# The delta net's transposed inverse factor, made by transposing instead of by a second product

## The chip, the core and the metric

The kernel runs on one core of one Trainium2 chip. The metric is device time in microseconds. The core's engines are named as the profile names them: PE is TensorE (PEld its weight loads), DVE VectorE, ACT ScalarE, POOL GpSimd, SP the queue that issues most DMAs. All data is float32.

## The reference, cut to what matters

The model is one block with a delta net and a gated linear attention, a mixture of experts, and two transformer layers, for 256 tokens and a context of 256 more. The change touches only the solve inside the delta net:

```python
kb = k * beta[..., None]
a = jnp.where(strict, jnp.einsum('nbhik,nbhjk->nbhij', kb, k) * decay, 0.0)
rhs = jnp.concatenate([v * beta[..., None], kb * jnp.exp(gcum)[..., None]], axis=-1)
sol = lax.linalg.triangular_solve(a, rhs, left_side=True, lower=True, unit_diagonal=True)
u, w = sol[..., :dv], sol[..., dv:]
```

So for each head and chunk the inverse of a unit triangular matrix, I + a, is applied to two right sides. The scan over the chunks then carries a state of 128x128 per head. It is done for 4 heads in two directions.

## The kernel before, in words

The kernel works with chunks of 128 tokens, so there are 4 chunks (two of the context, two of the sequence), 2 directions `d` and 4 heads. A step is `(d, s, phase)`: direction, place of the chunk in the scan, and one of ten phases. Four heads are always handled together: "a four" below is the four products of 128x128 by 128x128 that the helper `four` issues into one PSUM bank, or four transposes into one bank. Bank `AB[d]` (2 or 3) and bank `CD[d]` (4 or 5) belong to direction `d`.

The inverse is built by doubling. `B[0]` holds a block diagonal inverse X, and `B[3]` its transpose Y. Phase 1 makes both for blocks of 2. Each of phases 2 to 7 doubles the blocks:

- POOL masks the matrix into `B[4]` (line 1980, event `dn_am`).
- PE makes the four P = B4'B0 into `AB` (`dn_p`), and ACT copies it to `B[5]` (line 2195, `dn_p_copied`).
- PE makes the four "X product", B3'B5, into `AB` (`dn_x`, line 853, not in phase 7, where X is no longer needed), and the four "Y product", B5'B3, into `CD` (`dn_y`, line 854).
- DVE subtracts the X product from `B[0]` (line 1483, `dn_xs`) and the Y product from `B[3]` (line 1485, `dn_ys`).

Phase 0 makes the matrix (`dn_segments`, `dn_gram`, on DVE line 1443), phase 8 uses Y for w and u and the product with the state (`dn_w`, `dn_u`, `dn_ws`), phase 9 makes the state update and the output.

The order is written out by hand in `DN_SLOTS`: 44 slots; in slot t direction 0 is at phase t mod 10 and direction 1 four slots behind it. Below, slot (5,1) means direction 0 at phase 5 and direction 1 at phase 1. In a slot every engine does `delta_first` of direction 0, then of direction 1, then `delta_second` of each, then its `fill_slot`. Every engine works strictly in its own order. The fills are work of other parts that covers waits: projections of the layer's input on PE in slots 0 to 6 (512 or 256 columns a product, 7 us a slot), and on DVE convolutions in slots 1 and 2, a head norm in slot 3 and smaller pieces in 4 and 5. After slot 6 there is no fill, and with direction 0 finished in slot 39 the last four slots have direction 1 alone.

Phase 1 on DVE is four operations on SBUF operands in a row (lines 1191, 1449, 1191, 1453): X for blocks of 2, then its transpose. For s = 2 and 3 there are three more in `delta_second` (1191 three times), which make the score matrix of the output. POOL has one or two operations a slot and direction: the mask of line 1980, and products of keys, values or gates (line 1957) in phases 3, 5, 6 and 7.

All matrix products are recorded under line 501 and all transposes under line 513, the helpers' lines. All copies by ACT are under line 2010.

Of the kernel before, what the change touches and what calls it, by code (L numbers as in the profile page):

```python
# [20 lines left out]
ALU = mybir.AluOpType  # L21
# [12 lines left out]
H = 4  # L34
# [91 lines left out]
def dn_count(*phases, chunks=range(4)):  # L126

    steps = [step for slot in DN_SLOTS for step in slot if step[2] in phases and step[1] in chunks]
    return {step: i + 1 for i, step in enumerate(steps)}


DN_0, DN_1, DN_8, DN_9 = (dn_count(phase) for phase in (0, 1, 8, 9))
DN_1Q = dn_count(1, chunks=(2, 3))
# [112 lines left out]
def build(nc, A, out):  # L246
    with ExitStack() as ctx:
# [239 lines left out]
        def _(engine):  # L487
# [295 lines left out]
            def delta_first(step):  # L783
# [17 lines left out]
                elif phase < 8:  # L801
# [3 lines left out]
                    else:  # L805
                        engine.wait_ge(*pe.at("dn_x0", DN_1[d, s, 1]))
                        if s >= 2:
                            engine.wait_ge(*pe.at("dn_q3_copied", DN_1Q[d, s, 1]))
                    four(AB[d], d, lambda m, h: (B[4][:, m, :], B[0][:, m, :]), "dn_p")
                elif phase == 8:  # L810
                    engine.wait_ge(*pe.at("dn_ys", DN_LEVELS[d, s, 7]))
                    engine.wait_ge(*pe.at("dn_kb", DN_KB[d, s, 3]))
# [20 lines left out]
            def delta_second(step):  # L833
# [10 lines left out]
                elif 2 <= phase < 8:  # L844
                    engine.wait_ge(*pe.at("dn_p_copied", DN_LEVELS[step]))
                    if phase > 2:
                        engine.wait_ge(*pe.at("dn_ys", DN_LEVELS[d, s, phase - 1]))
                    else:
                        engine.wait_ge(*pe.at("dn_y0", DN_1[d, s, 1]))
                        if s >= 2:  # L850
                            engine.wait_ge(*pe.at("dn_q2_copied", DN_1Q[d, s, 1]))
                    if phase < 7:
                        four(AB[d], d, lambda m, h: (B[3][:, m, :], B[5][:, m, :]), "dn_x")
                    four(CD[d], d, lambda m, h: (B[5][:, m, :], B[3][:, m, :]), "dn_y")
                elif phase == 8 and s:
# [330 lines left out]
        def _(engine):  # L1186
# [247 lines left out]
            def delta_first(step):  # L1434
# [10 lines left out]
                elif phase == 1:  # L1445
# [6 lines left out]
                    engine.wait_ge(*v.last())  # L1452
                    tt(of(B[3], d), wide(ident), of(B[3], d), ALU.subtract).then_inc(*v.inc("dn_y0"))
                elif phase == 9 and s < 3:
                    engine.wait_ge(*v.at("dn_ds", DN_S[step]))
# [11 lines left out]
            def delta_second(step):  # L1467
# [12 lines left out]
                elif 2 <= phase < 8:  # L1480
                    if phase < 7:
                        engine.wait_ge(*v.at("dn_x", DN_XS[step]))
                        tt(of(B[0], d), of(B[0], d), ps(2 + d), ALU.subtract).then_inc(*v.inc("dn_xs"))
                    engine.wait_ge(*v.at("dn_y", DN_LEVELS[step]))
                    tt(of(B[3], d), of(B[3], d), ps(4 + d), ALU.subtract).then_inc(*v.inc("dn_ys"))  # L1485
                elif phase == 8 and s:
# [1026 lines left out]
```

## Time and profile before

| | us |
|---|---|
| median of 3 runs | 2779.77 |
| lowest and highest run | 2775.85, 2779.93 |
| span of the profiled execution, first to last instruction | 2773.7 |
| median of the runs less that span (start and end of the launch, and the spread between executions) | 6.1 |
| the delta net's 44 slots in the profile | about 302 to 556 |
| PE, DVE, ACT, POOL busy in the whole span | 92%, 40%, 21%, 4% |
| mean granted TensorE clock, as a share of full speed | 0.963 |

The page has no total of the profiled execution itself beside its span. Busy shares are averages over parts with different limits; what counts for this change is the stretch from 302 to 556 us. "PEclk" is the granted clock of TensorE: 1.00 is 2.4 GHz and 0.50 is 1.2 GHz. In the groups, the idle time behind a bar or in square brackets is the engine's idle time before the work, with what ended it.

### The profile page before, as it was taken

To read this page: it belongs to the slowest core of one execution; us is meant where nothing else is said; L and a number is where in the kernel's file an instruction comes from. 1 tells how busy PE (TensorE), PEld (TensorE's weight loads), DVE (VectorE), ACT (ScalarE), POOL (GpSimd) and SP (SyncE) were. 2 spreads that over 40 slices of the span, in tenths; PEclk is the share of its full clock that TensorE was granted. 3 is DMA by queue.
4 is the path that set the end of the run, shared out by engine and by line. 5 is a ranking of instruction groups with operands and counts; after the bars stand their busy time and mean duration, and the time that the engine had idled before them with its cause. 6 is when DMAs were issued, how large, how long until landed. Compare 5 with 4: busy or idle time off the path is not lost.

```text
span 2773.7 us, 37722 instructions
## 1 busy us (share of the span) xinstructions
PE 2550.8 (92%) x15259; PEld 1933.4 (70%) x15264; DVE 1103.4 (40%) x2325; ACT 585.4 (21%) x1032; POOL 115.3 (4%) x98
## 2 busy tenths in 40 slices
PE   5999889989799999979999779999999997799998
PEld 2686588868456655549948468699499484586993
DVE  1455445501311111136550831366666507312665
ACT  3632422210211111121011521110100105311000
POOL 0000144300000000000000000000000000000000
PEclk8999999999999999989999889999999998799999
DMA  7126100025499999974444004344344350043340
GB/s 280 62 79 278 54 31 1 1 108 211 157 414 422 422 422 422 422 309 173 178 147 173 30 1 182 152 166 184 142 162 176 144 196 31 1 182 152 153 168 15
DMA packets 74309, 485.50 MB, mean 175 GB/s; under 512 B 7872, under 2 KB 14528, under 8 KB 16704
## 3 DMA queue, kind: packets, MB, share of 16 engines
q1 hardware_dynamic: 65808, 472.46, 42.8%
q10 hardware_dynamic: 8368, 11.14, 1.2%
q8 instruction: 98, 1.61, 0.2%
q14 instruction: 35, 0.29, 0.0%
HBM read 479.38 MB, written 4.19 MB: 174 GB/s over the span
## 4 chain that ended last, share of the span: by engine, by line
PE 82%; DVE 7%; DMA 5%; ACT 3%; issue 2%; SPq 0%; ACTq 0%; DVEq 0%; POOL 0%; POOLq 0%
PE bank L501 80%; DMA ring<-in_stream 5%; ACT arena L2010 2%; PE bank L513 2%; DVE arena L1191 1%; DVE softmax_small L1881 1%; DVE arena L1879 1%; DVE arena L1902 0%; ACT hT L2010 0%; DMA bias_scratch<-arena 0%; ACT ring_late L2010 0%; DVE arena L1449 0%; ACT L2010 0%; DVE softmax_small L1889 0%; DVE arena L1485 0%
## 5 line engine op out<-in xcount | busy, mean ns | idle before, releaser
L501 PE MATMUL bank<-arena 128*128 128x128 f32 (+4 forms) x3864 | 619.5, 318 | 67.8 <-ACT arena L2010 43.1
L501 PEld LDWEIGHTS bank<-arena 128*128 128x128 f32 (+2 forms) x3864 | 485.4, 195 | 175.5 <-issue 87.0
L501 PE MATMUL bank<-hT,ring 128*128 128x256 f32 (+2 forms) x2144 | 463.3, 374 | 8.1 <-issue 6.7
L2010 ACT ACTIVATE arena<-bank 128x512 f32<-128x512 f32 (+2 forms) x384 | 218.0, 568 | 1156.7 <-PE bank L501 1131.2
L501 PEld LDWEIGHTS bank<-hT,ring 128*128 128x128 f32 x2144 | 357.5, 193 | 97.1 <-issue 64.7
L501 PE MATMUL bank<-ring,arena 128*64 128x256 f32 (+3 forms) x2184 | 298.6, 406 | 31.3 <-DMA ring<-in_stream 29.0
L501 PE MATMUL bank<-hT,ring_late 128*128 128x256 f32 (+1 forms) x1568 | 279.4, 336 | 6.7 <-issue 6.7
L501 PEld LDWEIGHTS bank<-ring,arena 128*64 128x64 f32 (+2 forms) x2184 | 176.4, 141 | 144.7 <-issue 82.7
L501 PEld LDWEIGHTS bank<-hT,ring_late 128*128 128x128 f32 x1568 | 248.9, 193 | 31.0 <-issue 7.5
L2010 ACT ACTIVATE hT<-bank 128x256 f32<-128x256 f32 (+2 forms) x92 | 38.6, 420 | 642.4 <-PE bank L501 471.3
L501 PE MATMUL bank<-arena,ring_late 128*128 128x128 f32 (+1 forms) x1088 | 157.4, 299 | 5.1 <-DVE arena L1485 2.8
L501 PE MATMUL bank<-ring_late,hT 128*64 128x512 f32 (+2 forms) x632 | 162.0, 584 | 0.0
L1191 DVE TENSOR_TENSOR arena<-arena 128x512 f32<-128x512 f32 (+5 forms) x55 | 33.7, 615 | 321.4 <-ACT arena L2010 320.8
L501 PEld LDWEIGHTS bank<-arena,ring_late 128*128 128x128 f32 x1088 | 144.2, 193 | 12.7 <-DVE arena L1485 3.6
L513 PE MATMUL bank<-constants,arena 128*128 128x128 f32 x492 | 87.1, 325 | 58.3 <-ACT arena L2010 44.5
L501 PE MATMUL bank<-arena,ring 128*128 128x128 f32 (+1 forms) x864 | 125.0, 299 | 11.5 <-issue 8.0
L513 PEld LDWEIGHTS bank<-constants,arena 128*128 128x128 f32 x492 | 68.1, 167 | 93.1 <-issue 58.0
L1191 DVE TENSOR_TENSOR arena<-arena,bank 128x512 f32<-128x512 f32 x16 | 11.0, 688 | 303.7 <-PE bank L501 303.7
L501 PEld LDWEIGHTS bank<-arena,ring 128*128 128x128 f32 x864 | 114.1, 195 | 17.7 <-issue 12.7
L501 PEld LDWEIGHTS bank<-ring_late,hT 128*64 128x64 f32 (+1 forms) x632 | 58.1, 147 | 87.8 <-issue 85.0
L501 PE MATMUL bank<-ring_late,arena 128*64 128x256 f32 (+2 forms) x680 | 115.7, 404 | 3.2 <-DVE arena L1513 2.3
L2001 POOL TENSOR_TENSOR x_tok<-x_tok,arena 128x512 f32<-128x512 f32 x8 | 11.8, 1492 | 2207.2 <-DVE arena L1802 2207.2
(215 smaller groups left out, 2239.1 us busy)
## 6 DMA issues: line engine op xcount, KB each, us to landing
ring<-in_stream SPq DMA_DIRECT2D x248, 1024.0 KB, 8.9
ring_late<-in_stream SPq DMA_DIRECT2D x198, 1024.0 KB, 10.4
arena<-bias_scratch ACTq DMA_DIRECT2D x4, 1536.0 KB, 18.0
bias_scratch<-arena ACTq DMA_DIRECT2D x12, 256.0 KB, 2.0
constants<-in_con SPq DMA_DIRECT2D x1, 1184.0 KB, 9.3
x_tok<-in_x SPq DMA_DIRECT2D x1, 1024.0 KB, 5.3
arena<-in_ctx SPq DMA_DIRECT2D x1, 1024.0 KB, 6.8
out<-x_tok SPq DMA_DIRECT2D x2, 512.0 KB, 2.7
```

The lines of the kernel that those rows point to most:

```text
L501: ins = engine.matmul(out_, lhsT, rhs, start=start, stop=stop, skip_group_check=True)
L513: ins = engine.transpose(out_, in_, ident[0:k, 0:k])
L1191: return tt(o, x, y, ALU.mult)
L1879: tt(e, src, bias2[:, m.bias], ALU.add).then_inc(*v.inc("sm_in"))
L1881: engine.tensor_reduce(stat(m, 0), e, AX.X, ALU.max).then_inc(*v.inc())
L2001: engine.tensor_tensor(x, x, ffU[j], ALU.add).then_inc(*g.inc("ff_joined"))
L2010: engine.activation(o, i, f, **kw).then_inc(*s_.inc(ev))
```

## The change

In phases 2 to 6 the Y product and its subtraction are gone. Instead, in phases 3 to 7 PE transposes X (`B[0]`, as the phase before left it) right behind the P product, with four transposes into bank `CD[d]`, and DVE copies the bank to `B[3]`. Phase 7 still has the Y product and its subtraction, which start from the transposed X. `DN_Y` numbers the events: `turned` for a transpose and its copy, `last` for the product of phase 7. The copy stands in DVE's `delta_first`, so it comes after what DVE's fill of the slot before has, and after what direction 0 has in `delta_first` when it belongs to direction 1.

```diff
+DN_Y = dn_y_count()
@@ PE, delta_first, phases 2 to 7
                     four(AB[d], d, lambda m, h: (B[4][:, m, :], B[0][:, m, :]), "dn_p")
+                    if phase > 2:
+                        if phase > 3:
+                            engine.wait_ge(*pe.at("dn_ys", DN_Y[d, s, phase - 1, "turned"]))
+                        for h in range(H):
+                            transpose(CD[d][:, 128 * h:128 * h + 128], B[0][:, 4 * d + h, :], ev="dn_y" if h == H - 1 else None)
                 elif phase == 8:
-                    engine.wait_ge(*pe.at("dn_ys", DN_LEVELS[d, s, 7]))
+                    engine.wait_ge(*pe.at("dn_ys", DN_Y[d, s, 7, "last"]))
@@ PE, delta_second, phases 2 to 7
                     if phase > 2:
-                        engine.wait_ge(*pe.at("dn_ys", DN_LEVELS[d, s, phase - 1]))
+                        engine.wait_ge(*pe.at("dn_ys", DN_Y[d, s, phase, "turned"]))
...
                     if phase < 7:
                         four(AB[d], d, lambda m, h: (B[3][:, m, :], B[5][:, m, :]), "dn_x")
-                    four(CD[d], d, lambda m, h: (B[5][:, m, :], B[3][:, m, :]), "dn_y")
+                    else:
+                        four(CD[d], d, lambda m, h: (B[5][:, m, :], B[3][:, m, :]), "dn_y")
@@ DVE, delta_first
+                elif 3 <= phase < 8:
+                    engine.wait_ge(*v.at("dn_y", DN_Y[*step, "turned"]))
+                    engine.tensor_copy(of(B[3], d), ps(4 + d)).then_inc(*v.inc("dn_ys"))
@@ DVE, delta_second
                         tt(of(B[0], d), of(B[0], d), ps(2 + d), ALU.subtract).then_inc(*v.inc("dn_xs"))
-                    engine.wait_ge(*v.at("dn_y", DN_LEVELS[step]))
-                    tt(of(B[3], d), of(B[3], d), ps(4 + d), ALU.subtract).then_inc(*v.inc("dn_ys"))
+                    else:
+                        engine.wait_ge(*v.at("dn_y", DN_Y[*step, "last"]))
+                        tt(of(B[3], d), of(B[3], d), ps(4 + d), ALU.subtract).then_inc(*v.inc("dn_ys"))
```

Later lines move: the products' line 501 is 511 after the change, the transposes' 513 is 523, DVE's subtractions 1483 and 1485 are 1502 and 1505, phase 1's 1191, 1449 and 1453 are 1207, 1465 and 1469, the convolution's 1335, 1337 and 1339 are 1351, 1353 and 1355, and the copy is 1472.

PE before, from the fill of slot 2 through slot 3 (direction 0 alone, phase 3) into the fill of slot 3, whose transposes wait for `pj_free`:

```order
L501 MATMUL bank<-hT,ring 128x512 x7
L501 MATMUL bank<-arena 128x128 [waits dn_xs,dn_am]
L501 MATMUL bank<-arena 128x128 x3
L501 MATMUL bank<-arena 128x128 [waits dn_ys,dn_p_copied]
L501 MATMUL bank<-arena 128x128 x7
L513 MATMUL bank<-constants,arena 128x128 [waits pj_free]
```

PE after, the same place:

```order
L511 MATMUL bank<-hT,ring 128x512 x7
L511 MATMUL bank<-arena 128x128 [waits dn_xs,dn_am]
L511 MATMUL bank<-arena 128x128 x3
L523 MATMUL bank<-constants,arena 128x128 x4
L511 MATMUL bank<-arena 128x128 [waits dn_ys,dn_p_copied]
L511 MATMUL bank<-arena 128x128 x3
L523 MATMUL bank<-constants,arena 128x128 [waits pj_free]
```

Four of the eight products behind the wait are gone, and four transposes stand between P and that wait.

DVE before, the end of slot 2's work and slot 3's (the second convolution, 1335 to 1339, is the fill of slot 2; the head norm follows):

```order
L1485 TENSOR_TENSOR arena<-arena,bank 128x512 [waits dn_y]
L1335 TENSOR_SCALAR ring_late<-ring_late,vectors 128x512 [waits pj_free]
L1337 SCALAR_TENSOR_TENSOR ring_late<-ring_late,vectors 128x2x255 [waits dve]
L1339 SCALAR_TENSOR_TENSOR ring_late<-ring_late,vectors 128x2x255 [waits dve]
L1483 TENSOR_TENSOR arena<-arena,bank 128x512 [waits dn_x]
```

DVE after:

```order
L1351 TENSOR_SCALAR ring_late<-ring_late,vectors 128x512 [waits pj_free]
L1353 SCALAR_TENSOR_TENSOR ring_late<-ring_late,vectors 128x2x255 [waits dve]
L1355 SCALAR_TENSOR_TENSOR ring_late<-ring_late,vectors 128x2x255 [waits dve]
L1472 COPY arena<-bank 128x512 [waits dn_y]
L1502 TENSOR_TENSOR arena<-arena,bank 128x512 [waits dn_x]
```

What the X product waits for (`dn_ys`) stood ahead of the convolution, and stands behind it now.

DVE before, slot (5,1): the end of slot (4,0), phase 1 of direction 1, and direction 0's subtractions of phase 5:

```order
L1485 TENSOR_TENSOR arena<-arena,bank 128x512 [waits dn_y]
L1191 TENSOR_TENSOR arena<-arena,constants 128x512 [waits dn_a]
L1449 TENSOR_TENSOR arena<-constants,arena 128x512 [waits dve]
L1191 TENSOR_TENSOR arena<-arena,constants 128x512 [waits dn_at_copied]
L1453 TENSOR_TENSOR arena<-constants,arena 128x512 [waits dve]
L1483 TENSOR_TENSOR arena<-arena,bank 128x512 [waits dn_x]
```

DVE after:

```order
L1472 COPY arena<-bank 128x512 [waits dn_y]
L1207 TENSOR_TENSOR arena<-arena,constants 128x512 [waits dn_a]
L1465 TENSOR_TENSOR arena<-constants,arena 128x512 [waits dve]
L1207 TENSOR_TENSOR arena<-arena,constants 128x512 [waits dn_at_copied]
L1469 TENSOR_TENSOR arena<-constants,arena 128x512 [waits dve]
L1502 TENSOR_TENSOR arena<-arena,bank 128x512 [waits dn_x]
```

Ahead of phase 1's four operations there is now a copy that waits for transposes of the same slot, where there was a subtraction of the slot before. In slot (1,7) the copy stands behind the four operations instead, and the Y product of direction 1 waits for it.

## Rows read from the trace of the kernel before

**Rows 1.** Busy time by stretch: us, busy (instructions) by engine, PEclk, DMA share, GB/s.
```profile
305.40:556.00 250.60, 225.47 (x1687) 204.07 (x1690) 131.60 (x204) 68.11 (x108) 96.36 (x76) 0.99 0.04 16
```
**Rows 2.** Groups by shape, 305 to 562 us: busy, mean ns | idle before.
```profile
L501 PE MATMUL bank<-arena 128*128 128x128 f32 x1288 | 162.3, 282 | 20.4 <-ACT arena L2010 13.5 <-DVE arena L1483 4.7 <-DVE arena L1489 0.8
...
L1459 DVE COPY arena<-bank 128x512 f32<-128x512 f32 x2 | 1.4, 692 | 1.5 <-PE bank L501 1.5
```
**Rows 3.** Timeline (start, length): four transposes, then a four of products.
```profile
385.59 0.60 PE L513 MATMUL bank<-constants,arena 128*128 128x128 f32 x4
386.02 1.06 PE L501 MATMUL bank<-arena 128*128 128x128 f32 x8
```
**Rows 4.** Timeline: two fours without a wait between them, ACT's copy of the first.
```profile
421.76 1.06 PE L501 MATMUL bank<-arena,ring_late 128*128 128x128 f32 x8
422.65 1.06 PE L501 MATMUL bank<-ring_late,arena 128*128 128x128 f32 x8
422.92 0.60 ACT L2010 ACTIVATE arena<-bank 128x512 f32<-128x512 f32 x1 [3.10 <-PE bank L501]
```
**Rows 5.** Timeline, direction 1 alone, phases 5 to 6.
```profile
539.65 0.60 ACT L2010 ACTIVATE arena<-bank 128x512 f32<-128x512 f32 x1 [4.88 <-PE bank L501]
540.30 3.16 PE L501 MATMUL bank<-arena 128*128 128x128 f32 x24 [0.75 <-ACT arena L2010]
541.50 0.69 DVE L1483 TENSOR_TENSOR arena<-arena,bank 128x512 f32<-128x512 f32 x1 [3.90 <-PE bank L501]
543.56 0.60 ACT L2010 ACTIVATE arena<-bank 128x512 f32<-128x512 f32 x1 [3.31 <-PE bank L501]
```
**Rows 6.** Timeline, slot 3: PE's P and products, the convolution's end on DVE.
```profile
325.86 1.05 PE L501 MATMUL bank<-arena 128*128 128x128 f32 x8
327.66 2.05 PE L501 MATMUL bank<-arena 128*128 128x128 f32 x16 [0.75 <-ACT arena L2010]
328.96 0.75 DVE L1339 SCALAR_TENSOR_TENSOR ring_late<-ring_late,vectors 128x510 f32<-128x510 f32 x1
329.55 1.04 PE L513 MATMUL bank<-constants,arena 128*128 128x128 f32 x8
```
**Rows 7.** Timeline, slot (5,1) of s = 2 into slot (6,2).
```profile
458.23 0.68 DVE L1191 TENSOR_TENSOR arena<-arena,constants 128x512 f32<-128x512 f32 x1
458.92 1.28 POOL L1980 TENSOR_TENSOR arena<-arena,constants 128x512 f32<-128x512 f32 x1 [2.53 <-PE bank L501]
458.94 1.80 DVE L1449 TENSOR_TENSOR arena<-constants,arena 128x512 f32<-128x512 f32 x1
463.79 0.67 DVE L1483 TENSOR_TENSOR arena<-arena,bank 128x512 f32<-128x512 f32 x1
464.61 10.30 PE L501 MATMUL bank<-arena 128*128 128x128 f32 x88 [1.19 <-DVE arena L1483]
```
**Rows 8.** Timeline, slots (1,7) and (2,8), direction 0 at s = 2.
```profile
438.79 0.69 DVE L1449 TENSOR_TENSOR arena<-constants,arena 128x512 f32<-128x512 f32 x1
440.12 1.64 DVE L1453 TENSOR_TENSOR arena<-constants,arena 128x512 f32<-128x512 f32 x1
443.61 0.68 DVE L1485 TENSOR_TENSOR arena<-arena,bank 128x512 f32<-128x512 f32 x1
444.34 1.16 PE L501 MATMUL bank<-arena,ring_late 128*128 128x128 f32 x8 [1.02 <-DVE arena L1485]
```
**Rows 9.** PE's two longest waits here, and PE by stretch (columns of rows 1).
```profile
335.37 3.24 PE L501 MATMUL bank<-arena 128*128 128x128 f32 x16 [2.04 <-ACT arena L2010]
410.12 11.81 PE L501 MATMUL bank<-arena 128*128 128x128 f32 x88 [2.96 <-DVE arena L1483]
...
411.20:414.60 3.40, 3.40 (x18) 0.51 0.00 0
414.60:418.00 3.40, 3.40 (x33) 1.00 0.02 5
```
**Rows 10.** PE in a stretch with 16 transposes of v, fill of slot 5.
```profile
350.52 1.04 PE L513 MATMUL bank<-constants,ring_late 128*128 128x128 f32 x8
350.00:360.00 10.00, 9.69 (x79) 1.00 0.03 13
```

More of the change, by code:

```diff
@@ L129, in dn_count, with dn_y_count @@
     return {step: i + 1 for i, step in enumerate(steps)}
+def dn_y_count():
+    order = []
+    for slot in DN_SLOTS:
+        order += [(*step, "turned") for step in slot if 3 <= step[2] < 8]
+        order += [(*step, "last") for step in slot if step[2] == 7]
+    return {key: i + 1 for i, key in enumerate(order)}
+DN_Y = dn_y_count()
 DN_0, DN_1, DN_8, DN_9 = (dn_count(phase) for phase in (0, 1, 8, 9))
```

## The prediction, made before the change was run

> **What bounds the kernel now.** The busy shares come first, and mislead a little: PE is busy for 92% of the whole span, so less PE work looks like a gain. The change acts only in the delta net, so I read the stretch of its slots. From 305.4 to 556 us PE is busy for 225.5 of 250.6 us [rows 1]. The groups by shape say what ended PE's idle time there: 13.5 us ACT's copies of P, 4.7 us DVE's X subtraction, all before products of this solve [rows 2]. So PE is the bound where both directions have work, and the chain P, copy, X product, subtraction, next P is the bound where one direction has nothing beside it. The timeline gives that chain's lengths, and the windows the clock.
>
> **The steps, from rows.** A four of products takes PE 0.89 us (421.76 to 422.65), and its reader starts 1.16 after its start on ACT [rows 4] and 1.20 on DVE after a wait of PE (540.30 to 541.50) [rows 5]. A four that PE has waited for takes 0.1 more. A four of transposes takes PE 0.43 (385.59 to 386.02) and is 4 records where a four of products is 8 [rows 3]. I take 0.20 from the end of a four to DVE's start, which is 1.20 less 0.99, and 0.05 from the end of a copy to PE (539.65 + 0.60 to 540.30) [rows 5], 0.15 from the X subtraction (463.79 + 0.67 to 464.61) [rows 7]. DVE's copy of a bank takes 0.69 [rows 2], as its subtraction does [rows 5]. DVE's busy time therefore stays: 40 subtractions go and 40 copies come.
>
> Removed on PE: phases 2 to 6, 4 chunks, 2 directions, 40 fours of 0.89, 35.6 us. Added: phases 3 to 7, 40 fours of 0.43, 17.2 us. PE does 18.4 us less. That would be the gain if PE never waited.
>
> On the transposes' price the Trainium skill (TensorE: Matmul & The Clock Gate, Terms) says that TensorE's transpose mode is four times faster for FP32. By that a four would take 0.22 and PE would save 8 us more; the row shows a factor of two, and the row is used.
>
> **What the new order costs.** The X product waits for the copy of the transposed X, and that starts only when P and the transposes are through. P to X alone was 1.81 (1.16 + 0.60 + 0.05). After a wait it becomes 0.99 + 0.43 + 0.20 + 0.69 + 0.05 = 2.36. Behind X nothing of its own follows any more: before, Y's 0.89 covered the subtraction. Now X to the next P of that direction is 1.20 + 0.69 + 0.15 = 2.04, of which X itself covers 0.99. So the Y product's time comes back as a wait wherever the other direction has no four behind X.
>
> Slot by slot, in 3 turns of 10 slots, a first part with fills and a tail:
>
> 1. Slots 2 to 6, where PE is full of fills. Slot 2 loses Y: -0.89. In slot 3 DVE's copy stands behind the convolution of the fill, which ends at 329.71 (328.96 + 0.75) [rows 6]. It follows an ACT copy at the end of PE's fill, so it moves with PE to 328.8; copy and start put X at 329.55, its end at 330.45. Before, X and Y ended at 329.44. That is +1.0 in sum, +1.9 for the slot. Slots 4 and 5 wait for ACT, which is busy with other work, longer than for the copy, and lose Y: -0.89 each. Slot 6 loses two Y and gains one four of transposes: -1.35. Together -2.1.
> 2. Slots (8,4), (9,5), (0,6): the other direction's fours stand behind X, so the Y product's 0.89 is gained and 0.43 to 0.48 paid: -0.45, -0.3, -0.4. Three turns and one more (8,4): -3.9.
> 3. Slots (3,9) and (4,0): X is last, own P is next. Saved 0.89, paid 0.43 for the transposes and 1.05 of wait less the 0.1 to 0.3 that is there now: +0.45 each, 6 of them: +2.8.
> 4. Slot (5,1) into (6,2). DVE's phase 1 begins after the copy. From P of phase 5 (about 457.7, 1.2 ahead of POOL's start) to P of phase 6 it is 6.9 now, of which phase 1 takes 5.56 (458.23 to 463.79) [rows 7]. It then begins 2.31 after P instead of 0.5. Its length depends on POOL: where POOL starts during it the second operation takes 1.80 [rows 7], where not 0.69, and the four take 3.7 (0.72 more than 438.79 to 441.76) [rows 8]. Starting later, it meets less of POOL's two operations. I take 5.0 between 3.7 and 5.6, nearer to the collided row because POOL's second operation of the slot is then still running. P of phase 6 comes at 2.31 + 5.0 + 0.82 = 8.1 (6.8 to 8.7), +1.2; slot (6,2) does 1.35 less work and waits 0.15 more. Net 0.0 a turn, between -1.3 and +0.6.
> 5. Slots (1,7), (2,8). Direction 1's copy stands behind phase 1 of direction 0, its Y product behind the copy. For s = 1 the last subtraction came right after phase 1; now copy 0.74 and Y 1.19 stand between, +1.9, less the 0.89 of Y in slot (2,8): +1.0. For s = 2, 3 three more DVE operations cover Y (441.76 to 443.61) [rows 8]: +0.65 for the copy in DVE's queue, less 0.89: about 0. PE waits here anyway (1.02 at 444.34).
> 6. Slot (7,3): two fours of transposes for one Y: +0.1 in each of 4.
> 7. The tail, direction 1 alone, phases 5 to 7: a step is 3.91 (539.65 to 543.56) [rows 5] and becomes 2.36 + 2.04 = 4.4. Three steps: +1.4.
>
> Sum: -2.1 - 3.9 + 2.8 + 0.0 + 1.0 + 0.4 + 1.4 = -0.4.
>
> **The clock.** In this stretch it fell twice to 1.2 GHz, after PE had waited 2.04 and 2.96. In the 3.40 us behind the second wait PE did 18 records where it does 33 at 2.4 GHz [rows 9]: 15 records of 0.111, 1.7 us. It did not fall after 1.19 [rows 7]. The change lengthens waits: slot 3 to about 3.2, slot (1,7) of s = 1 to 2.7, slot (6,2) to about 4.2 and 2.4 for s = 1 and 2. I take one fall more, +1.7; none to three is possible, 0 to +5.
>
> The forecast is +1.3 on the profiled span of 2773.7. The median of the runs is 6.1 above that span, and nothing outside the stretch changes, so 2779.77 + 1.3 = 2781.1. What a measurement of this kernel tells from no change is 0.2%, 5.6 us, so the forecast is no change that can be seen: the 18.4 us go into waits.
>
> **Rivals.**
>
> PE's time counts (faster). For it: PE is 90% busy in the stretch. Against: the waits that appear are in the chain of each direction. If phase 1 takes its shortest 3.7 in slot (5,1), and the (3,9) and (4,0) waits are half of what I say, the sum is -0.4 - 3.9 - 1.5 = -5.8 without a further fall: 2774. With every one of the 40 exchanges paying its 0.46 it would be -18.4, 2761; the tail alone excludes that.
>
> Phase 1 on DVE is the bound (slower). The place is slot (5,1) into (6,2), where the copy pushes phase 1 back while it still collides with POOL at 5.6 us, and the slots (1,7), where the copy stands behind it. The price is +0.6 a turn, 1.8, and a fall of the clock after each of the longer waits, three instead of one, 3.4 more: +6.5, 2786. It decides from two falls more than I count. For it: waits of 2.04 were enough once. Against: a shorter wait in slot (5,1) of s = 3 (no keys' product on POOL).
>
> The transposes let the clock fall (slower). If PE at transposes were as good as idle for the clock, each wait would grow by the 0.43 to 0.87 of transposes beside it and the waits of about 1 us would reach the 2.04 after which it fell. Five more falls are +8.5, with -0.4 that is 2788. Against: the stretch of 10 us with the 16 transposes of v had the clock at 1.00 throughout [rows 10], though they were only a fifth of its records. The Trainium skill (TensorE: Matmul & The Clock Gate, Part 4: PE-mode transpose) has this rule: transpose mode does not count as busy for the clock gate in the same way.
>
> **How the numbers follow.** The forecast has 0.50, "PE's time counts" 0.22, "phase 1 is the bound" 0.21, the transposes' clock 0.07. Of the 0.22 some 0.13 lie more than 5.6 us below, since its price of 5.8 is just at that bound. Of the 0.21 some 0.18 lie above it, all of the 0.07, and 0.05 of the forecast's own upper edge. So faster by over 0.2% 0.13, within 0.2% 0.57, slower 0.30. The range begins where phase 1 is shortest, the waits of item 3 are halved and one of the two falls of the clock goes too: 2779.77 - 5.8 - 1.7 = 2772.3, and ends with the transposes' clock at 2788 and 1 us beyond: 2772 to 2789. The forecast's own range is 2775 to 2785.
>
> **What would show it.** PE's busy time from 305 to 556 falls by 17 to 19 us and its idle time grows by as much. The transposes' group grows by 160 records at 0.11 of pitch. In slot 3 PE waits about 3 us for DVE's copy behind the convolution. The tail's step is 4.4. In slot (5,1) phase 1 starts 2.3 after P. PEclk shows three or four falls in the stretch. I am wrong if the transposes take 0.89, if the X product waits for ACT as before, or if the clock falls six times.

## The result, and the profile after

| | before | changed |
|---|---|---|
| median | 2775.62 us (20 runs, 2773.29 to 2779.93) | 2781.23 us (20 runs, 2776.31 to 2785.35) |
| ratio to before | 1 | 1.0018, interval 1.0012 to 1.0025 |
| span of the profiled execution | 2773.7 us | 2780.5 us |

The forecast of 2781.1 us was met. Its step was not: it was made as 1.3 us over a median of 3 runs, 2779.77, and in the 20 runs before has a median of 2775.62. The measured step is about +5 us (0.0018 x 2775.6; the two medians are 5.6 apart), with an interval of +3.3 to +6.9. What had to be explained is therefore not whether the sum was near, but where some 4 us more came from.

TensorE's groups by shape, 305 to 568 us of the changed kernel (they answer [rows 2]):

```profile
L511 PE MATMUL bank<-arena 128*128 128x128 f32 x974 | 135.1, 289 | 37.8 <-DVE arena L1472 17.5 <-DVE arena L1502 17.1 <-ACT arena L2030 2.3
L523 PE MATMUL bank<-constants,arena 128*128 128x128 f32 x232 | 35.4, 286 | 1.9 <-ACT arena L2030 1.9
```

The products before which PE was idle for 20.4 us [rows 2] are now ones before which it is idle for 37.8. ACT's copy of P, which ended 13.5 us of it, ends 2.3; the new copy of the transposed factor (L1472) ends 17.5 and the subtraction of X (L1502), which the Y product used to cover, 17.1 (4.7 before). The work removed has come back as two waits. VectorE's groups in the same stretch show that it has as many operations as before, 40 copies and 40 subtractions (and the 8 of phase 7):

```profile
L1472 DVE COPY arena<-bank 128x512 f32<-128x512 f32 x40 | 27.6, 690 | 55.3 <-PE bank L523 55.2
L1502 DVE TENSOR_TENSOR arena<-arena,bank 128x512 f32<-128x512 f32 x40 | 27.4, 684 | 32.5 <-PE bank L511 32.5
```

PE by stretch (the columns of [rows 1]): first the delta net's slots, then one fall of the clock, the 3.4 us behind it, and a long fall in the tail.

```profile
305.40:562.80 257.40, 215.84 (x1525) 191.51 (x1525) 127.72 (x204) 69.58 (x109) 94.06 (x76) 0.95 0.05 17
...
390.80:394.20 3.40, 3.40 (x20) 3.40 (x20) 0.69 (x1) 0.17 (x1) 0.18 (x1) 0.60 0.00 0
394.20:397.60 3.40, 2.53 (x23) 2.37 (x22) 0.69 (x1) 1.62 (x3) 2.08 (x2) 1.00 0.00 0
550.80:561.00 10.20, 8.55 (x40) 7.88 (x39) 1.38 (x2) 1.45 (x3) 0.00 (x0) 0.51 0.01 2
```

The slots have 162 records fewer than in [rows 1] (160 by the change, 40 x 8 less 40 x 4), yet end 6.8 us later. Of these 6.8 us, 5.3 arise in the solve and 1.5 ahead of it (below). In the window of [rows 1], 305.4 to 556 us, PE is busy for 210.6 us instead of 225.5: 14.9 less, where 17 to 19 were said, since work at 1.2 GHz takes longer. The first of the short stretches is mostly at 1.2 GHz (0.60 on the mean), the one behind it at 2.4; the last is at 1.2 GHz for all of its 10.2 us.

The timeline of the changed kernel at the places the prediction speaks of: slot 3 (answers to [rows 6]), the slots (0,6) and (1,7) of s = 1, slot (5,1) of s = 1 (to [rows 7]), the first P behind slot (2,8) of s = 1, and the tail (to [rows 5]).

```profile
329.58 0.75 DVE L1355 SCALAR_TENSOR_TENSOR ring_late<-ring_late,vectors 128x510 f32<-128x510 f32 x1
330.25 0.69 DVE L1472 COPY arena<-bank 128x512 f32<-128x512 f32 x1
331.08 1.13 PE L511 MATMUL bank<-arena 128*128 128x128 f32 x8 [3.11 <-DVE arena L1472]
...
380.36 1.28 ACT L2030 ACT_TABLE_LOAD   x1 [2.69 <-PE bank L511]
382.35 1.12 DVE L1459 SCALAR_TENSOR_TENSOR arena<-bank,arena 128x128 f32<-128x128 f32 x4 [2.21 <-ACT arena L2030]
383.39 0.68 DVE L1472 COPY arena<-bank 128x512 f32<-128x512 f32 x1
384.22 1.13 PE L511 MATMUL bank<-arena 128*128 128x128 f32 x8 [1.73 <-DVE arena L1472]
386.22 1.13 PE L511 MATMUL bank<-arena 128*128 128x128 f32 x8 [0.44 <-DVE arena L1502]
388.04 1.63 DVE L1469 TENSOR_TENSOR arena<-constants,arena 128x512 f32<-128x512 f32 x1
389.60 0.68 DVE L1472 COPY arena<-bank 128x512 f32<-128x512 f32 x1
390.43 3.51 PE L511 MATMUL bank<-arena 128*128 128x128 f32 x16 [2.64 <-DVE arena L1472]
...
397.49 1.13 PE L511 MATMUL bank<-arena 128*128 128x128 f32 x8 [0.87 <-DVE arena L1502]
...
407.15 1.13 PE L511 MATMUL bank<-arena 128*128 128x128 f32 x8 [1.01 <-DVE arena L1502]
409.36 0.82 DVE L1207 TENSOR_TENSOR arena<-arena,constants 128x512 f32<-128x512 f32 x1
...
413.82 0.68 DVE L1502 TENSOR_TENSOR arena<-arena,bank 128x512 f32<-128x512 f32 x1
414.64 1.19 PE L511 MATMUL bank<-arena 128*128 128x128 f32 x4 [3.92 <-DVE arena L1502]
...
545.96 1.13 PE L511 MATMUL bank<-arena 128*128 128x128 f32 x8 [0.87 <-DVE arena L1502]
548.41 1.13 PE L511 MATMUL bank<-arena 128*128 128x128 f32 x8 [0.88 <-DVE arena L1472]
550.41 1.91 PE L511 MATMUL bank<-arena 128*128 128x128 f32 x8 [0.87 <-DVE arena L1502]
```

In slot 3 and in (1,7) the copy starts as soon as the operation ahead of it in DVE's queue is through, and PE waits 3.11 and 2.64 us for it. In (0,6) of s = 1 it is behind the four operations of L1459 (1443 before), which make the matrix of the new chunk and themselves wait for ACT; and ACT is late because it first loads a table, 1.28 us. No other turn has such a load: in (0,6) of s = 2 the copy starts 0.20 us behind the transposes and X waits 0.88. In (5,1) phase 1 begins 2.21 us after P. The tail's step is 4.45 us (545.96 to 550.41), with two waits of 0.87 in it.

### The profile page after: what moved, and what is told of

It is laid out like the page before. It is cut to its first block, busy times and chain, and to the rows that moved or that the text cites. A ratio compares the mean times of both kernels' runs of the same rounds, so it can differ in the third digit from the quotient of the medians.

```text
span 2780.5 us, 37408 instructions
## 1 busy us (share of the span) xinstructions
PE 2543.8 (91%) x15104; PEld 1920.9 (69%) x15104; DVE 1100.1 (40%) x2325; ACT 585.1 (21%) x1032; POOL 113.0 (4%) x98
## 4 chain that ended last, share of the span: by engine, by line
PE 83%; DVE 8%; ACT 3%; DMA 3%; issue 2%; SPq 0%; ACTq 0%; DVEq 0%
PE bank L511 81%; DMA ring<-in_stream 3%; PE bank L523 2%; ACT arena L2030 2%; DVE arena L1207 1%; DVE softmax_small L1901 1%; DVE arena L1899 1%; DVE arena L1922 0%; DVE arena L1472 0%; DVE arena L1502 0%; ACT hT L2030 0%; DMA bias_scratch<-arena 0%; ACT ring_late L2030 0%; ACT L2030 0%; DVE arena L1465 0%
## 5 line engine op out<-in xcount | busy, mean ns | idle before, releaser
L511 PE MATMUL bank<-arena 128*128 128x128 f32 (+4 forms) x3544 | 591.7, 323 | 85.2 <-ACT arena L2030 32.3
L511 PEld LDWEIGHTS bank<-arena 128*128 128x128 f32 (+2 forms) x3544 | 455.3, 197 | 196.7 <-issue 111.4
L523 PE MATMUL bank<-constants,arena 128*128 128x128 f32 x652 | 111.1, 313 | 59.3 <-ACT arena L2030 43.5
L523 PEld LDWEIGHTS bank<-constants,arena 128*128 128x128 f32 x652 | 87.5, 161 | 93.0 <-issue 58.3
```

The lines of the kernel that those rows point to most:

```text
L511: ins = engine.matmul(out_, lhsT, rhs, start=start, stop=stop, skip_group_check=True)
L523: ins = engine.transpose(out_, in_, ident[0:k, 0:k])
```

## The experiments

All read the solve in one way. It is cut at the first product of phase 8 of a direction (the groups with `arena,ring_late` as operands, [rows 4] shows one at 421.76): from P of direction 0, phase 2, s = 0 to its phase 8 ("start"), from there from one phase 8 of direction 0 to the next (three turns), and from the last to phase 8 of direction 1 ("tail"). The falls of the clock to 1.2 GHz in each part are in brackets, read from windows of 0.4 us.

| solve in us | start | turn 1 | turn 2 | turn 3 | tail | sum |
|---|---|---|---|---|---|---|
| before | 54.66 (1) | 51.80 (1) | 52.99 | 56.48 | 18.82 | 234.75 |
| before, second profile | 54.66 (1) | 51.81 (1) | 52.98 | 56.49 | 18.82 | 234.76 |
| e12, before and busy | 54.03 | 50.31 | 52.98 | 56.49 | 18.83 | 232.64 |
| changed | 52.87 (1) | 55.46 (2) | 53.91 (1) | 55.63 | 22.18 (long) | 240.05 |
| e10, changed, second profile | 53.24 (1) | 54.19 (1) | 53.90 (1) | 55.64 | 20.07 | 237.04 |
| e2, Y kept in the tail | 53.26 (1) | 54.16 (1) | 53.91 (1) | 55.62 | 19.00 | 235.95 |
| e3, changed and busy | 54.24 (1) | 52.80 | 52.56 | 55.62 | 20.07 | 235.29 |
| e1, 19 places | 51.31 | 49.57 | 51.94 | 54.96 | 18.99 | 226.77 |
| e11, 19 places, second profile | 51.31 | 50.98 (1) | 51.97 | 54.98 | 19.00 | 228.24 |
| e5, the other 21 | 55.26 (1) | 56.42 (2) | 54.03 | 57.29 | 19.89 | 242.89 |
| e7, 22 places | 50.76 | 49.58 | 51.96 | 54.96 | 19.00 | 226.26 |
| e8, 22 places and busy | 51.78 | 49.58 | 51.95 | 54.96 | 19.00 | 227.27 |
| e4, identity | 54.53 (1) | 60.26 (2) | 56.39 | 59.52 | 21.90 | 252.60 |
| e6, turned twice | 56.68 (2) | 59.02 (2) | 56.26 | 59.33 | 21.82 | 253.11 |

Parts without a fall repeat to 0.03 us from one profile to another and between kernels that are alike there (the start, where transfers and fills run, to 0.4). So a term can be read part by part.

One difference lies ahead of the solve, in work that no edit touches. P of phase 2 starts at 315.30 and 315.05 us in the two profiles of before, and at 316.82 and 316.53 in those of the changed kernel, 1.5 later. About half of it is a fall of the clock near 300 us, before and changed:

```profile
301.60:304.60 3.00, 2.33 (x18) 1.85 (x16) 0.00 (x0) 2.94 (x4) 0.00 (x0) 1.00 0.33 87
...
301.60:304.60 3.00, 3.00 (x6) 1.28 (x5) 0.00 (x0) 2.16 (x3) 0.00 (x0) 0.50 0.00 0
```

All twelve other profiles have that fall, e12 too, whose solve is that of before. So it isn't the exchange that brings it; what does is not shown.

**e1 and e5: the two halves of the change.** Both name the set of places; phases outside it keep the Y product of the phase before.

```diff
+DN_TURN = {(d, s, p) ... if (d == 1 and p <= 6 and not (s == 3 and p == 6)) or (d == 0 and p == 7)}   # e5: not (...)
-                    if phase > 2:
+                    if step in DN_TURN:
                         ... transpose(CD[d][:, 128 * h:128 * h + 128], B[0][:, 4 * d + h, :], ...)
-                    else:
+                    if dn_product(step):       # phase 7, or the next phase is not in DN_TURN
                         four(CD[d], d, lambda m, h: (B[5][:, m, :], B[3][:, m, :]), "dn_y")
```

> The transposes stand only where the other direction's products lie behind X or where PE waits anyway: direction 1 in phases 3 to 6 (not in phase 6 of s = 3) and direction 0 in phase 7, 19 of the 40 places; elsewhere the Y product stays as before. Theory 'waits by place' (the order of the work decides): each turn keeps the -0.3 to -0.45 of slots (8,4), (9,5), (0,6) and loses the +0.45 of (3,9) and (4,0) and the +1.4 of the tail; about -2 a turn, -5 to -8 us against before (0.2 to 0.3%), -10 to -13 against the changed kernel where the falls of the clock go too. Theory 'clock': the waits of 2.6 and 3.9 us of s = 1 (direction 0 in slots (1,7) and (5,1)) are here too wherever the copy stands ahead of phase 1 on DVE, so at least two falls stay, and it is -2 to -4 against before. Theory 'transposes do not count for the clock': 19 places instead of 40, so about half of the changed kernel's extra falls, 0 to +2 against before.

> The complement of the kernel with 19 places: the transposes stand only in the other 21 (direction 0 in phases 3 to 6, direction 1 in phase 7 and in phase 6 of s = 3). If what each place costs adds up, this one is at the changed kernel less the 19 places: with 2781.2 for the changed kernel, 2775.1 for before and 2768.2 for the 19 places, +13 against before, 2788. By the waits alone (without the clock) the prediction's terms give less: +2.8 for (3,9) and (4,0), +1.0 for slot (1,7), +1.4 for the tail, -2.1 for the fills, so +3 and with three more falls of the clock +8. Under +3 would say that the gain of the 19 places isn't theirs.

Measured: e1 2768.18 us, ratio 0.9972 (0.9962 to 0.9982); e5 2785.63 us, ratio 1.0032 (1.0021 to 1.0043). One half is faster than before by 0.28%, the other slower by 0.32%. The ratios add up to +0.0004 where both together have +0.0018; with intervals of 0.0010 and 0.0011 to either side of the two, that is no clear difference. In the solve the parts without falls tell more: with before at 231.6 (e12 less 1.0, see there) e1 is at -4.9 and e5, its three falls taken off at 1.4 to 1.65 each, at +6.8; together +1.9, and the changed kernel is at +1.0 (below). So the halves add up to within 1 us. Of e1's 6.9 us, 4.9 are the order of the work. Its profile has no fall in the solve where before has two, worth 3.1 us, and lost 1.5 ahead of the solve. e5 is 9.1 us above the before of its runs, between the +8 of the waits with three falls and the +13 of the sum of places. PE in e1 by stretch, and two of its waits on the timeline:

```profile
330.00:360.00 30.00, 26.32 (x178) 23.62 (x177) 15.56 (x28) 13.53 (x17) 11.88 (x9) 1.00 0.17 63
...
405.00:425.00 20.00, 17.04 (x144) 16.27 (x144) 11.76 (x18) 4.18 (x7) 10.80 (x9) 1.00 0.00 1
...
336.90 2.05 PE L529 MATMUL bank<-arena 128*128 128x128 f32 x16 [2.04 <-ACT arena L2048]
...
409.06 5.04 PE L529 MATMUL bank<-arena 128*128 128x128 f32 x40 [2.96 <-DVE arena L1520]
```

It has the same two waits, 2.04 and 2.96 us, after which the clock fell in before [rows 9], and no fall. The expectation of the theory 'clock' that at least two falls stay was wrong.

**e9, e10, e11: the same kernels again.** No edit.

> The kernel before, profiled a second time. Theory 'a wait of that place brings the fall': the clock falls again at 336 and 411 us and nowhere else between 305 and 556. Theory 'the fall is chance from one execution to the next': other places, or one or none.

> The changed kernel, profiled a second time. Theory 'place': falls at 332, 390, 414, 469 and a long one from 551 in the tail. Theory 'chance': three or fewer of the five are at the same places; then the 5 us of clock in the first profile are one draw and not the mean price.

> The kernel with 19 places, profiled a second time. Theory 'place': no fall between 305 and 556 us, though it has the waits of 2.04 and 2.96 us after which the clock fell in the profile of before. Theory 'chance': one or two falls there.

Single runs: 2775.68, 2785.01 and 2770.83 us. Before fell at the same two places. The changed kernel fell at three of the five. The kernel with 19 places fell once, after the wait of 2.96. The stretches 388 to 405, 405 to 425, 465 to 480 and 530 to 558 us of the changed kernel's first profile, then of its second:

```profile
388.00:405.00 17.00, 12.83 (x90) 11.92 (x91) 6.38 (x9) 3.58 (x7) 6.52 (x6) 0.90 0.00 0
405.00:425.00 20.00, 14.63 (x110) 13.68 (x109) 11.53 (x17) 3.63 (x7) 10.47 (x9) 0.91 0.00 1
...
465.00:480.00 15.00, 12.99 (x98) 12.62 (x98) 9.99 (x14) 2.99 (x5) 7.34 (x6) 0.89 0.01 1
...
530.00:558.00 28.00, 22.86 (x165) 21.16 (x166) 9.64 (x14) 4.78 (x8) 7.62 (x7) 0.87 0.01 1
```

```profile
388.00:405.00 17.00, 12.64 (x98) 11.45 (x98) 7.43 (x13) 3.71 (x7) 7.02 (x6) 1.00 0.00 0
405.00:425.00 20.00, 14.75 (x110) 14.20 (x111) 11.25 (x15) 3.58 (x6) 10.06 (x8) 0.91 0.00 1
...
465.00:480.00 15.00, 13.00 (x99) 12.56 (x98) 8.85 (x12) 3.67 (x7) 6.91 (x6) 0.89 0.01 1
...
530.00:558.00 28.00, 22.07 (x180) 20.42 (x179) 9.66 (x14) 5.96 (x10) 6.43 (x6) 1.00 0.01 1
```

So a fall has places where it comes in some executions and not in others; what decides it there is not shown. The fall at 390 costs 24.08 - 22.65 = 1.43 us (phase 8 of direction 0, s = 0, to phase 8 of direction 1, in the two profiles), the one of e11 1.41, the long one in the tail 22.18 - 20.07 = 2.11. Against before, the falls beyond its two cost 4.3 us in the first profile of the changed kernel and 1.2 in the second (240.05 and 237.04, less 232.65 without falls, see e3, less the 3.15 that before's two cost).

**e3 and e12: the clock kept up, the waits left.** e3 is the changed kernel with zeros in its waits; e12 has `DN_TURN` empty, so every Y product is as before, and zeros in two places.

```diff
+            def keep_busy(n):
+                for _ in range(n):
+                    mm(bank[0][:, :], zero[:, 0:128], zero[:, :], start=True, stop=True)
+            WARM_FIRST = {9: 3, 10: 3, 11: 8, 19: 3, 20: 3, 21: 3, 29: 3, ...}     # e12: none
+            WARM_LAST = {15: 12, 25: 8, 35: 5, 39: 3, 40: 3, 41: 3, 42: 3}         # e12: {15: 10, 25: 4}
             for t, slot in enumerate(DN_SLOTS):
+                if t == 7:
+                    engine.wait_ge(*pe.at("pj_free", state["tile"]))
                 for step in slot:
                     delta_first(step)
+                keep_busy(WARM_FIRST.get(t, 0))
                 for step in slot:
                     delta_second(step)
                 fill_slot(t)
+                keep_busy(WARM_LAST.get(t, 0))
```

> The changed kernel, and PE does 71 more products in its waits (bf16, zeros times zeros, 128x128 by 128x512, into a bank that is free there), about 0.21 us each, in the slots with a wait of over 0.8 us. Nothing is computed with them. Theory 'clock': the waits stay and only PE's clock is kept at 2.4 GHz; the 24 us at 1.2 GHz between 305 and 566 us become under 8, which is -3.5 to -5 us against the changed kernel, about equal to before. Theory 'waits by place': 71 products of 0.21 are 15 us of PE; those behind which no wait is left cost time, so 0 to +4 against the changed kernel. The granted clock of the stretch tells it also without the time.

> The kernel before, with 10 products of zeros in PE's wait of 2.96 us at the end of slot (5,1) of s = 1 and 4 in that of s = 2. No wait is changed. Theory 'clock': the fall at 411 us goes, the other (336) stays, -1.7 us. It is also the measure of how much of the 6.9 us of the 19 places is clock: if this gives -1.7, two falls are 3.4 of them and the order of the work 3.5. Theory 'waits by place': 0, and all 6.9 are the order's.

Measured: e3 2775.46 us, ratio 1.0004 (0.9995 to 1.0013), by the ratios 3.9 us below the changed kernel; e12 2774.61 us, ratio 0.9996 (0.9987 to 1.0005). The wait at slot 7 that the zeros need costs 1.02 us in the start (e8 against e7: 51.78 and 50.76), in both. The same stretches as above in e3, from 388 us on:

```profile
388.00:405.00 17.00, 14.35 (x108) 12.14 (x107) 7.43 (x11) 4.18 (x7) 7.39 (x6) 1.00 0.00 1
405.00:425.00 20.00, 17.22 (x134) 14.75 (x133) 11.98 (x18) 4.12 (x7) 10.07 (x8) 1.00 0.01 2
...
465.00:480.00 15.00, 14.65 (x119) 13.16 (x117) 8.77 (x13) 4.47 (x8) 7.71 (x7) 1.00 0.01 1
...
530.00:558.00 28.00, 26.49 (x196) 21.44 (x195) 8.64 (x13) 4.79 (x9) 5.37 (x5) 1.00 0.00 1
```

Each of the four stretches with zeros in its waits is at 2.4 GHz. In two of them, 388 to 405 and 530 to 558, e10 had no fall either; the falls at 413 and 468 were in all three profiles of these waits without zeros (changed, e10, e2). Turn 1 goes from 54.19 to 52.80, turn 2 from 53.90 to 52.56 against e10, while turn 3, which had no fall, is as long as without zeros: 55.62 and 55.64. That is the clean measure: 1.39 and 1.34 us a fall, nothing for the zeros. The changed kernel without a fall is then, with the start of e10 less 1.65 for its fall (54.66 against 54.03 - 1.02), 51.6 + 52.80 + 52.56 + 55.62 + 20.07 = 232.65. Before without a fall is 232.64 - 1.02 = 231.6. **The order alone is +1.0 us**, known to the 0.4 of the start. In e12 turn 1 is 1.49 shorter as expected; the fall at 336 went too, though nothing was placed there and its wait of 2.04 us is the same. The median is only 1.0 lower, with an interval that takes in 0: the solve is 2.1 shorter, but 1.3 were lost ahead of it (P at 316.57 instead of 315.30).

**e2: the tail.**

```diff
+DN_TURN = {(d, s, p) ... if not (d == 1 and s == 3 and p >= 6)}
```

> The changed kernel, but in the tail (direction 1 alone, s = 3, phases 6 and 7 get their transposed factor by the Y product of the phase before, as in before). Theory 'waits by place': two steps of the tail go from 4.44 us back to 3.91, -1.0 us against the changed kernel. Theory 'clock': in the profile of the changed kernel the clock was at 1.2 GHz for 10.2 us from 550.9 on, and PE's work in it cost about 4 us more; with waits of 0.75 and 0.86 us between fours of three it stays at 2.4 GHz there, as before, and the run is -3 to -5 against the changed kernel. Theory 'transposes do not count for the clock': the same -3 to -5, but a fall remains where the tail's first step still has its transposes.

Measured: 2777.74 us, ratio 1.0008 (0.9999 to 1.0017), 3.5 below the changed kernel by the medians and 2.8 by the ratios. The tail is 19.00 where e10 without a fall has 20.07: the two steps cost 1.07, as expected. The profile shows it:

```profile
542.48 3.13 PE L529 MATMUL bank<-arena 128*128 128x128 f32 x24 [0.88 <-DVE arena L1490]
546.35 3.16 PE L529 MATMUL bank<-arena 128*128 128x128 f32 x24 [0.75 <-ACT arena L2048]
550.26 1.16 PE L529 MATMUL bank<-arena 128*128 128x128 f32 x8 [0.75 <-ACT arena L2048]
```

The step is 3.91 again and there is no fall in the tail, but e10 had none either: the 1.07 is shown to be the tail's waits, and that the rest is a fall that comes in some executions is likely, not shown.

**e4 and e6: does the mode of PE matter to the clock?** e4 replaces the transposes by products with the identity, e6 does each twice over.

```diff
-                        for h in range(H):
-                            transpose(CD[d][:, 128 * h:128 * h + 128], B[0][:, 4 * d + h, :], ...)
+                        four(CD[d], d, lambda m, h: (B[0][:, m, :], ident), "dn_y")      # e4
+                        for r in range(2):                                              # e6
+                            for h in range(H):
+                                transpose(CD[d][:, 128 * h:128 * h + 128], B[0][:, 4 * d + h, :], ...)
```

> The changed kernel, with its 40 fours of transposes done as fours of products with the identity: the same result, reader and waits, but 8 records and 0.89 us instead of 4 and 0.43, and PE in its ordinary mode. Theory 'transposes do not count for the clock': the falls go although the waits stay, so under 10 us at 1.2 GHz between 305 and 566 us instead of 24; the time is 40 x 0.46 = 18.4 less what waits absorb, less 4 to 6 for the clock: +2 to +8 against the changed kernel. Theory 'waits by place' and 'clock by waits': the falls stay, since the waits do; +8 to +18 against the changed kernel, because P, product with the identity, copy and X are one chain.

> The changed kernel with each of its 40 fours of transposes done twice over into the same bank: 8 records and 0.87 us on PE, as the products with the identity had (8 records, 0.89), with the same waits and readers; only PE's mode differs from that kernel, which took 2795.9 us. Theory 'transposes do not count for the clock': PE looks idle in 0.87 us more beside each wait, so the clock is at 1.2 GHz for longer than the identity kernel's 27 us between 300 and 600 us, also in the tail, where the identity kernel had no fall, and the time is 3 to 8 us above 2795.9. Theory 'the work counts, whatever its mode': the same falls and 2794 to 2797.

Measured: e4 2795.89 us, ratio 1.0069 (1.0056 to 1.0083); e6 2794.11 us, ratio 1.0059 (1.0045 to 1.0073). The two agree in the parts without a fall (56.39 and 56.26 in turn 2, 59.52 and 59.33 in turn 3, 21.90 and 21.82 in the tail), so eight records of transposes are eight records of products in time. Four stretches of e4, then of e6, and one more of e6:

```profile
330.00:360.00 30.00, 26.09 (x169) 23.54 (x170) 16.44 (x29) 13.52 (x17) 10.52 (x9) 0.94 0.15 58
...
388.00:405.00 17.00, 13.33 (x97) 12.46 (x95) 7.72 (x11) 3.58 (x6) 5.11 (x4) 0.90 0.00 0
405.00:425.00 20.00, 14.13 (x90) 13.15 (x91) 9.13 (x14) 3.30 (x6) 8.71 (x8) 0.83 0.00 1
...
465.00:480.00 15.00, 12.17 (x98) 11.10 (x97) 9.79 (x15) 4.18 (x7) 6.86 (x6) 1.00 0.00 0
```

```profile
330.00:360.00 30.00, 27.07 (x168) 24.62 (x168) 14.66 (x26) 13.53 (x17) 11.21 (x9) 0.89 0.11 36
...
388.00:405.00 17.00, 13.49 (x99) 12.62 (x97) 7.58 (x10) 3.58 (x6) 5.12 (x4) 0.90 0.00 0
405.00:425.00 20.00, 13.92 (x99) 12.76 (x99) 9.52 (x15) 3.58 (x6) 9.65 (x9) 0.91 0.00 1
...
465.00:480.00 15.00, 12.15 (x97) 10.93 (x96) 10.51 (x16) 3.99 (x8) 7.68 (x7) 1.00 0.00 0
...
569.00:572.40 3.40, 3.40 (x19) 3.40 (x18) 0.00 (x0) 0.80 (x2) 0.00 (x0) 0.50 0.00 0
```

In the solve both were at 1.2 GHz for four lengths of 3.4 us, most of them in the same places, and neither in turn 2, where the changed kernel fell in both of its profiles and e2 too. If transposes left PE as good as idle for the clock, e6 should have fallen there. It did not, and it took no longer than e4. So the strong form of the rule of the Trainium skill (TensorE: Matmul & The Clock Gate, Part 4: PE-mode transpose), that transpose mode doesn't count for the gate as products do, is not borne out by this pair.

A weaker form stays open, for the tail speaks the other way. e6 fell at 569.0, 0.4 us behind the end of its tail; e4, with products in the same waits, not before 581.9, 12 us behind. Between 305 and 600 us e6 was at 1.2 GHz for 27.3 us and e4 for 23.9. Over all runs, of the four profiles that have transposes in the last two steps of the tail and no zeros (changed, e10, e5, e6) three fell in it or within 0.4 us behind it, e10 not; of the nine with products there none fell until 11 us behind. That is no test: all of the nine but e4 also have shorter or fewer waits there.

The other lesson is the price: PE's work grew by 40 x 0.46 = 18.4 us and the time by 14.7, as one expects where P, transposes, copy and X are one chain; in how many of the 40 places they are was not counted.

**e7 and e8: three places more.** `DN_TURN` of e1 `or (d == 0 and s == 0 and p >= 4)`; e8 adds the zeros of e12.

> The 19 places (2768.2 us) and three more: direction 0 in phases 4, 5 and 6 of s = 0, whose slots wait for ACT longer than the copy takes (2.04 and 1.33 us). Not phase 3, whose copy stands behind the convolution on DVE. Theory 'waits by place': the Y products of slots 3, 4 and 5 go, -0.89 each, and 0.43 of transposes in slot 6 comes: -2.2, 2766.0. Theory 'clock': slot 4's wait grows by 0.4 to 0.9 us with PE doing less around it, a fall there is likelier; 2766 to 2768.5.

> The 22 places, and 10 products of zeros (bf16, 0.21 us each) on PE in the wait of 2.96 us at the end of slot (5,1) of s = 1 and 4 in the 1.18 us of s = 2. Nothing is computed with them. Theory 'clock': where that wait was followed by a fall in some executions, there is none now: 0 to -1.7 against the 22 places without them, and a narrower spread of the runs. Theory 'waits by place': the products end before DVE's subtraction releases PE, 0.

Measured: e7 2767.96 us, ratio 0.9966 (0.9952 to 0.9979); e8 2771.64 us, ratio 0.9974 (0.9963 to 0.9986). e7 is not to be told from e1. The start is only 0.55 shorter, where -2.2 was expected. PE on the timeline of e7:

```profile
330.89 1.13 PE L529 MATMUL bank<-arena 128*128 128x128 f32 x8 [0.76 <-DVE arena L1520]
...
350.63 1.13 PE L529 MATMUL bank<-arena 128*128 128x128 f32 x8 [0.97 <-DVE arena L1520]
```

The new waits of 0.76 and 0.97 are for the subtraction of X (L1520): the Y product had covered it here too, ahead of the next P. In e8 the zeros cost nothing behind slot 7 (49.58, 51.95, 54.96 and 19.00, as in e7). Its median says little about them: three of its seven runs are at 2765.5 to 2767.1 and four at 2771.6 to 2773.7. The narrower spread that was expected did not come.

## Why the prediction was right in its number and short in its step

The number was met by luck: two errors of about 4 us, in the base and in the step, cancelled (last points below). Its sum by parts, each without falls of the clock, against what was measured (before from e12, changed from e3 and e10; the parts add up to -0.5, the prediction's -0.4 has 2.8 for six times 0.45):

| part | predicted | measured |
|---|---|---|
| start (item 1, first (7,3)) | -2.0 | -1.4 |
| turn 1 (items 2 to 6, s = 1) | +0.85 | 52.80 - 50.31 = +2.5 |
| turn 2 | -0.15 | 52.56 - 52.98 = -0.4 |
| turn 3 | -0.15 | 55.62 - 56.49 = -0.9 |
| tail (item 7, last (8,4)) | +0.95 | 20.07 - 18.83 = +1.2 |
| sum | -0.4 | +1.0 |

- **The mechanism held.** The saved 18.4 us of PE went into waits for the copy and for the subtraction of X. Slot 3's wait was given as about 3.2 and is 3.11; the tail's step as 4.4 and is 4.45; slot (1,7) of s = 1 as 2.7 and is 2.64; phase 1 in slot (5,1) starts 2.21 after P, 2.3 was said, and P to P there is 7.49 where 8.1 was taken out of 6.8 to 8.7.
- **Two terms of turn 1 were mis-sized.** The timelines of e12 and e3, cut at products:

| turn 1 | predicted | measured |
|---|---|---|
| slots (8,4), (9,5) | -0.75 | 9.56 - 10.06 = -0.5 |
| slot (0,6), to P of phase 7 | -0.4 | 6.97 - 6.01 = +1.0 |
| slot (1,7), to phase 8 of direction 1 | +1.9 | 6.11 - 4.71 = +1.4 |
| slot (2,8), to P of phase 3 | -0.9 | 3.82 - 3.81 = 0.0 |
| slots (3,9), (4,0) | +0.9 | 9.66 - 8.70 = +1.0 |
| slot (5,1) | +1.2 | 7.49 - 6.89 = +0.6 |
| slots (6,2), (7,3) | -1.1 | 9.19 - 10.13 = -0.9 |

- **Item 2, the slot (0,6) of s = 1**, is 1.4 off. It was put at -0.4 as in the other turns. There DVE's queue holds the operations of L1459 ahead of the copy, they wait for ACT behind its table load of 1.28 us, and X waits 1.73 instead of the 0.88 of turn 2; P of phase 7 then waits 0.44 for the subtraction of X. The load was there in before too, at 381.13. The order of DVE's queue was read for slot 3 and slot (1,7), but not for this one, and three turns were taken as alike.
- **Item 5, slot (2,8) of s = 1**, is 0.9 off. Its Y product was counted as a gain of 0.89, but the next P waits 0.87 for the subtraction of X (397.49 above): it stands last in its slot, as in item 3. The slots (1,7) and (5,1) cost 0.5 less each than was said, which hid a part of both errors.
- **The clock.** "One fall more" is what the second profile shows (3 against 2, +1.2 us). The first has 4 and a long one in the tail, +4.3. Judging by the length of a single wait failed: the tail fell after waits of only 0.87, and before's 2.04 and 2.96 went without a fall in e1. Its price of 1.7 a fall is 1.34 to 1.65 in the runs, since PE waits for a part of the 3.4 us anyway.
- **The sum of both** is +2.3 (second profile) to +5.3 (first) in the solve, against +1.3 predicted. With the 1.5 ahead of the solve, of which the prediction had nothing ("nothing outside the stretch changes"), it is +3.8 to +6.8, and the runs have about +5.
- **The base.** A median of 3 runs, two of them at 2779.8, stood for before. That alone put the forecast 4 us too high, and the shortfall of the step took it back.
- **The rivals.** "PE's time counts" is out for the whole change, but in 19 of its places 4.9 of the 8.7 us saved come out as time (e1). "Phase 1 on DVE is the bound" had the sign right, and the falls behind the lengthened waits, which e3's zeros remove; its price in slot (5,1) itself was not found, P to P grew by 0.6 where 1.2 was in the forecast already. "The transposes let the clock fall" had falls in the tail right; its reason is against e6 in turn 2, and open in the tail.

What stays open: behind the solve (the span less the start of phase 8 of direction 1) most profiles have 2222.2 to 2224.8 us, but e10 has 2783.2 - 553.57 = 2229.6 and e3 2779.6 - 551.56 = 2228.0, with the clock at 1.2 GHz for 194 and 191 us from 560 us on, where both profiles of before have 174. The solve is over by then. What decides this was not settled. It may be what makes two groups some 5 us apart in the runs of before, e3 and e8; that is not shown, since each has profiles of one group only. Also not tried: the 19 places less those of slot (0,6) of s = 1, where X waits 1.72 in e1 too, and its turn 1 up to phase 8 of direction 1 is 0.8 longer than in before (21.53 and 20.77).

## What to carry to other kernels

A product whose result isn't needed at once may still be worth its time, because it covers the operation that another engine does meanwhile: before it is removed, ask of each place what PE does in its stead. The same exchange made the program 7 us shorter in the 19 places where other work stood behind X or PE waited anyway, and 9 us longer in the other 21 (by the order of the work alone, -4.9 and +6.8); apply it by place. Before a copy is added to a queue, read what stands ahead of it there in every slot, not in the typical one: a table load in one turn of three was enough. And take the base of a small step from more than three runs.

## What the runs showed of the hardware

- A fall of the clock after the same wait is not certain. PE's wait of 2.96 us had a fall behind it in three of five profiles (both of before and e11, not e1 and e7), the wait of 2.04 us in two of five (both of before, not e12, e1 and e11). Waits of 0.87 us, two in each 4.45 us, had a fall of 10.2 us behind them once out of twice.
- With products of zeros in the waits (bf16, 0.21 us each) TensorE stayed at 2.4 GHz in each of four stretches of one profile; in two of them it had fallen in every profile without zeros. They cost nothing where they ended ahead of the release; each fall less was worth 1.34 to 1.49 us.
- Four transposes of 128x128 f32 take 0.43 us, four products 0.89, and twice four transposes as long as the products: 21.82 and 21.90 us in the tail.
- A table load on ACT took 1.28 us, and one of them held up a chain that ran through ACT, DVE and PE.
